# Turning attention probabilities by a product with a scaled diagonal, built on GpSimd

## The chip, the core and the metric

The kernel runs on one core of one Trainium2 chip. A core has five engines that run their own instruction streams and meet only through semaphores: PE (TensorE, matrix products; its weight loads are shown apart as PEld), DVE (VectorE), ACT (ScalarE), POOL (GpSimd) and SP (SyncE, which here only issues DMAs). The metric is the device time of one execution in microseconds; lower is better.

## What is computed

Two transformer blocks follow each other on 512 tokens of width 1024, all in float32. The second block holds the attention that this case is about. It has 16 query heads in 4 groups and three branches for each head: over 31 compressed keys ("c"), over selected blocks ("s") and over a window ("w"). With 512 tokens and 8 blocks of which 8 are chosen, "s" is plain causal attention, and "w" is causal attention with some padding keys. The core of it, from the reference:

```python
p_s = masked_softmax(s_s, key_pos <= t[:, None])
o_s = jnp.einsum('bghqkl,bgqkld->bghqd', p_s..., v_g)
...
p_w = masked_softmax(s_w, mask_w)
o_w = jnp.einsum('bghqk,bgkd->bghqd', p_w.astype(q_b.dtype), v_b)
return g_b[..., 0:1] * o_c + g_b[..., 1:2] * o_s + g_b[..., 2:3] * o_w
```

So every row of probabilities is an exponential, divided by its row sum, times a gate of that token, head and branch.

## The kernel before

The large matrix products (lines 888 to 890) split each float32 operand into two parts and take three products. They fill most of the time. The attention of the second block runs between 1661 and 1864 us of the span, in one software pipeline over the names "N0", "N1" and "X" (X is a cross attention that follows). N0 and N1 have two iterations each, and an iteration has 36 steps: 4 "c" steps, then 16 "s" and 16 "w" steps. A step is one head and one tile of 128 queries (`qt` from 0 to 3); its row is `e.n = 128 * (qt + 1)` keys wide, so widths of 128, 256, 384 and 512 come four steps each, twice per iteration. That makes 32 such steps and 80 chunks of 128 keys per iteration, 128 steps and 320 chunks in all.

What a step does, and on which engine:

- `score` (lines 743 to 748, PE): the product of q and k into a PSUM bank. Two heads stand next to each other in the array.
- `dve_attention`, first half (lines 841 to 849, DVE): adds the mask and takes the row's maximum, into `Sm` in SBUF.
- `act_attention` (lines 788 to 796, ACT): the exponential in place, with the row sum into `st[:, 12 + c]`.
- `dve_attention`, second half (lines 863 to 872, DVE), one step behind the first half: for "w" the padding's share is added to the sum (line 863), then the reciprocal (line 865), then line 872 multiplies the whole row of `Sm` by the reciprocal and by the gate, and increments `s_norm`.
- `turned_over` (lines 750 to 761, PE): waits for `s_norm`, turns each chunk of `Sm` with `pe.transpose` against the identity `ident` (a part of the tile `cst`) into one of two PSUM banks, and increments `t_full`.
- `act_attention` (line 813, ACT): copies the turned chunks to `PTnr` in SBUF.
- `values` (lines 763 to 767 and 1095, PE): the product with v, for two heads at once.

The order on PE is written out by hand: for each pair of steps, two scores, then a turn and a product with v, then a second turn and perhaps a second product with v. The turns stand three steps behind the scores (`lag_of` gets the whole name "N0" here, which isn't in "ANX"). `Sm` is a ring of six rows. POOL has nothing to do between its clearing of `PTc` (line 568) and the fetch of `xT` back from memory (line 572), which waits for the start of X.

Of the kernel before, what the change touches and what calls it, by code (L numbers as in the profile page):

```python
# [20 lines left out]
ACT = mybir.ActivationFunctionType  # L21
# [86 lines left out]
def build(nc, a, out):  # L108

    ctx = ExitStack()  # L110
    with ctx:
# [151 lines left out]
        ng = place("ng", [P, TT, 48])  # L263
        ngT = place("ngT", [48, T], at=S_at)
# [171 lines left out]
        bias_ready, pair_ready = sem("bias_ready"), sem("pair_ready")  # L436
# [61 lines left out]

        @block.gpsimd
        def _(pool):  # L500
            pool.memset(ones[:, :], 1.0).then_inc(pool_cst, 1)
            pool.memset(eps[:, :], EPS).then_inc(pool_cst, 1)
            pool.memset(kcT[:, :, :], 0.0).then_inc(pool_cst, 1)
            pool.memset(vcp[:, :, :], 0.0).then_inc(pool_cst, 1)

            pool.memset(diag[:, 0, 0:2], 0.0).then_inc(sq_used, 2)
            pool_squares(pool, 0)
            pool_squares(pool, 1)
            pool.wait_ge(cst_in, 16)

            for h in range(8 + 2):
                if h >= 2:
                    b = bias4[(h - 2) % 4]
                    if h < 6:

                        pool.wait_ge(o_free, O_RING + attn_at["B"]["O0"])
                    else:

                        pool.wait_ge(s_masked, attn_at["B"]["S0"] + 8 * ((h - 4) // 2))
                    pool.wait_ge(bias_in[h % 2], 16 * (h // 2))  # L520
                    pool.tensor_tensor(b[:, :], bias_raw[:, h % 2, :], C("mask_chunk"), ALU.add).then_inc(bias_ready, 1)
                if h < 8:
                    if h >= 2:

                        pool.wait_ge(bias_ready, h - 1)
                    pool.dma_start(bias_raw[:, h % 2, :], a["rel"][h]).then_inc(bias_in[h % 2], 16)
            pool_squares(pool, NORM["ffn2"])

            pool.wait_ge(sq_ready, 8 * NORM["final"] + 1)
            for m, a_ in enumerate((acc, acc_g)):  # L530
                pool.memset(a_[:, :], 0.0).then_inc(acc_zero, 1)
                pool.wait_ge(acc_zero, NORM["final"] + 1 + m)
            with pool.Fori(0, DC) as i:
                for s, a_ in enumerate((acc, acc_g)):
                    pool.wait_ge(sq_ready, i * 2 + (8 * NORM["final"] + s + 1))

                    pool.wait_ge(sq_used, i * 2 + (8 * NORM["final"] + s + 2))
                    pool.tensor_tensor(a_[:, :], a_[:, :], sqb[s][:, :], ALU.add).then_inc(sq_used, 1)

            pool.wait_ge(h_tmp, 8)  # L540
            pool.dma_start(spill, xT[:, :, :].rearrange("p c t -> p (c t)")).then_inc(spilled, 16)

            for m, n in enumerate("kv"):
                pool.dma_start(w1c[m][:, :, :], a[f"w_cmp_{n}1_2"][0].rearrange("(m p) n -> p m n", p=P)).then_inc(cmp_in, 16)
                pool.dma_start(w2c[:, m, :, :], a[f"w_cmp_{n}2_2"][0].rearrange("(c p) n -> p c n", p=P)).then_inc(cmp_in, 16)

            for m in range(2):
                for g in range(4):
                    pool.wait_ge(mm_free[2 * m + g // 2], 1 + stages["kc"]["m0"][2 * m + g // 2] + 1)
                    src = kcv[64 * (g % 2):64 * (g % 2) + 64, 2 * m + g // 2, :]  # L550
                    pool.dma_start(Z[m][0:64, g, :], src).then_inc(z_in[m], 16)
                    pool.dma_start(Z[m][64:128, g, 0:T - 1], src[:, 1:T]).then_inc(z_in[m], 16)

            pool.wait_ge(vc_done, 1)
            for m in range(2):
                pool.memset(wrg[m][:, :, :], 0.0).then_inc(wrg_zero, 1)
            pool.wait_ge(wrg_zero, 2)
            for m, n in enumerate("ai"):
                w = a[f"w_rg_{n}_2"][0].rearrange("(c b) i j -> b i c j", b=2)
                for b in range(2):  # L560
                    pool.dma_start(wrg[m][64 * b:64 * b + 64, :, 64 * b:64 * b + 64], w[b]).then_inc(rg_in, 16)


            pool.wait_ge(y1_done, DC)
            for h in range(4):
                if h:
                    pool.wait_ge(qz_zero, h)
                pool.memset(PTc[h][:, :], 0.0).then_inc(qz_zero, 1)

            pool.wait_ge(pv_done, PV_RING + attn_at["X"]["M0"])  # L570
            pool.wait_ge(spilled, 16)
            pool.dma_start(xT[:, :, :].rearrange("p c t -> p (c t)"), spill).then_inc(spill_back, 16)
            pool_squares(pool, NORM["g_mlp"])
            j = NORM["g_final"]
            pool.wait_ge(sq_ready, 8 * j + 1)
            pool.memset(acc[:, :], 0.0).then_inc(acc_zero, 1)
            pool.wait_ge(acc_zero, j + 1)
            for c in range(DC - 1):
                pool.wait_ge(sq_ready, 8 * j + c + 1)
                pool.wait_ge(sq_used, 8 * j + c + 2)  # L580
                pool.tensor_tensor(acc[:, :], acc[:, :], sqb[c % 2][:, :], ALU.add).then_inc(sq_used, 1)


        class Order:


            def __init__(self, eng, sem_):
                self.eng, self.sem, self.n, self.i, self.per = eng, sem_, 0, None, 0

            def __call__(self, ins):  # L590
                ins.then_inc(self.sem, 1)
                self.n += 1
                self.eng.wait_ge(self.sem, self.n if self.i is None else self.i * self.per + self.n)

            def loop(self, n, per, body):

                if n < 3:
                    for i in range(n):
                        at = self.n
                        body(i)  # L600
                        assert self.n == at + per, (self.n - at, per)
                else:
                    at = self.n
                    with self.eng.Fori(0, n) as i:
                        self.i, self.per = i, per
                        body(i)
                        assert self.n == at + per, (self.n - at, per)
                    self.i, self.n = None, at + n * per

        def full(S, b, i):  # L610

            return i + (S["m0"][b] + 1)

        def free_before(S, b, i):

            return i + (S["m0"][b] + 1)

        def free_after(S, b, i):

            return i + (S["m0"][b] + 2)  # L620

        def act_split(act, S, s, i):

            if S["name"] == LAST and isinstance(i, int) and i == S["its"] - 1:
                return
            act.wait_ge(w_raw[s], i * 16 + 16 * (S["k0"] + 2))
            if S["rel"][s] is None:
                act.wait_ge(slot0_used, i + (S["s0"] + 1))
            else:
                act.wait_ge(mm_full[S["rel"][s]], full(S, S["rel"][s], i))  # L630
            act.activation(whi[s][:, :], wraw[s][:, :], ACT.Copy).then_inc(w_hi[s], 1)  # L631

        def dve_split(dve, S, s, i):

            if S["name"] == LAST and isinstance(i, int) and i == S["its"] - 1:
                return
            dve.wait_ge(w_hi[s], i + (S["k0"] + 2))
            dve.tensor_tensor(wlo[s][:, :], wraw[s][:, :], f32(whi[s][:, :]), ALU.subtract).then_inc(w_lo[s], 1)  # L638

# [83 lines left out]

        def steps(names):

            at = [(n, i, t) for n in names for i in range(attn_at[n]["its"]) for t in range(attn_at[n]["n"])]  # L730
            bank0 = PREP[{"A": "ak", "B": "bk", "C": "cq", "N0": "kk"}[names[0]]][1]
            return [Step(n, i, t, k, bank0) for k, (n, i, t) in enumerate(at)], lag_of(names[0])

        def pe_attention(pe, names, q_of, k_of, v_of, turn, chunk_of):
# [16 lines left out]
            def turned_over(e):  # L751

                pe.wait_ge(s_norm, e.s + 1)
                pe.wait_ge(t_free, e.u + 1)
                if e.m == "c":
                    for q in range(TT):
                        mm = pe.transpose(e.tbank[0:NC32, q * P:(q + 1) * P], e.Sm[:, q * NC32:(q + 1) * NC32], ident)
                else:
                    for kc in range(e.n // P):
                        mm = pe.transpose(e.tbank[:, kc * P:(kc + 1) * P], e.Sm[:, kc * P:(kc + 1) * P], ident)  # L760
                mm.then_inc(t_full, 1)
# [1563 lines left out]
```

## Time and profile before

| what | value |
|---|---|
| median of 3 runs | 2375.66 us (2374.99 to 2376.89) |
| time of the profiled execution | 2375.66 us |
| span of the profiled execution, first to last instruction | 2373.5 us |
| mean granted TensorE clock | 0.983 of full speed |
| PE, PEld, DVE, ACT, POOL busy, share of the span | 96%, 76%, 52%, 41%, 6% |
| one iteration of the 36 steps, from the chain | 46.34 us, four of them |

The span leaves out 2.2 us ahead of the first and behind the last instruction. Busy time of PE counts each product from its start to its modelled end, and products overlap; so the distance from one start to the next is what a product costs, not its duration.

### The profile page before, as it was taken

The numbers are of one execution on the slowest core, as the hardware profiler recorded it, in microseconds if no ns is written. First come the engines' busy times: TensorE is split into PE (matmuls) and PEld (weight loads), VectorE is DVE, ScalarE is ACT, GpSimd is POOL, SyncE is SP. The second block draws the span as 40 slices with busy tenths as digits, with TensorE's granted clock in tenths as the row PEclk, the third lists the DMA queues.
The fourth block names the chain that finished last, engine by engine and source line by source line (L and its number), as shares of the span: only waits on it lengthen the run. The fifth ranks groups of instructions, "written<-read, shape, count | busy, mean of one in ns | idle before, by whom it ended". The sixth has DMA issues, their size and how long they took to land.

```text
span 2373.5 us, 29956 instructions
## 1 busy us (share of the span) xinstructions
PE 2276.7 (96%) x10990; PEld 1805.0 (76%) x10990; DVE 1235.4 (52%) x2245; ACT 976.4 (41%) x1620; POOL 147.7 (6%) x119
## 2 busy tenths in 40 slices
PE   7999999989889999999999999999999999999998
PEld 6888888757667777888888877687555788888887
DVE  6444436674545455434434656743899655432432
ACT  6332224454555333433223422633788544321322
POOL 2000002101000000100001420000000001000011
PEclk9999999989899999999999999999999999999999
DMA  6322323212101223232322372122000232333231
GB/s 234 106 90 87 107 92 102 98 54 64 61 27 54 80 98 106 89 106 83 112 88 76 102 250 70 61 92 75 2 2 2 72 107 95 100 91 104 89 106 54
DMA packets 213615, 206.81 MB, mean 87 GB/s; under 512 B 4848, under 2 KB 194544, under 8 KB 213264
## 3 DMA queue, kind: packets, MB, share of 16 engines
q1 hardware_dynamic: 210512, 192.31, 25.6%
q0 software_dynamic: 3008, 13.24, 1.7%
q8 instruction: 59, 0.97, 0.2%
q14 instruction: 36, 0.29, 0.0%
HBM read 199.25 MB, written 4.19 MB: 86 GB/s over the span
## 4 chain that ended last, share of the span: by engine, by line
PE 82%; DVE 8%; ACT 5%; issue 3%; DMA 1%; POOL 0%; ACTq 0%; SPq 0%; DVEq 0%; POOLq 0%
PE ps L888 25%; PE ps L890 25%; PE ps L889 25%; DVE Sm L843 2%; DVE wlo L638 2%; PE ps L748 2%; PE ps L760 2%; ACT whi L631 2%; PE ps L1095 1%; DMA wraw<-in_w_in 1%; DVE st L865 1%; PE ps L1087 1%; PE ps L1135 1%; PE ps L1160 1%; DVE Sm L872 0%
## 5 line engine op out<-in xcount | busy, mean ns | idle before, releaser
L888 PE MATMUL ps<-hH,whi 128*128 128x512 f32 x1528 | 600.8, 393 | 15.6 <-DVE wlo L638 13.8
L638 DVE TENSOR_TENSOR wlo<-wraw,whi 128x2048 fp32r<-128x2048 f32 x192 | 440.4, 2294 | 324.0 <-ACT whi L631 324.0
L890 PE MATMUL ps<-hH,wlo 128*128 128x512 f32 x1528 | 596.0, 390 | 0.0
L889 PE MATMUL ps<-hL,whi 128*128 128x512 f32 x1528 | 595.8, 390 | 0.0
L631 ACT ACTIVATE whi<-wraw 128x2048 fp32r<-128x2048 f32 x192 | 366.8, 1911 | 436.4 <-PE ps L890 428.6
L888 PEld LDWEIGHTS ps<-hH,whi 128*128 128x128 f32 x1528 | 287.1, 188 | 83.6 <-issue 14.5
L889 PEld LDWEIGHTS ps<-hL,whi 128*128 128x128 f32 x1528 | 287.0, 188 | 61.3 <-issue 1.4
L890 PEld LDWEIGHTS ps<-hH,wlo 128*128 128x128 f32 x1528 | 287.0, 188 | 60.8
L888 PE MATMUL ps<-gH,whi 128*128 128x512 f32 x608 | 237.2, 390 | 0.0
L889 PE MATMUL ps<-gL,whi 128*128 128x512 f32 x608 | 236.6, 389 | 0.0
L890 PE MATMUL ps<-gH,wlo 128*128 128x512 f32 x608 | 236.6, 389 | 0.0
L888 PE MATMUL ps<-whi,hH 128*128 128x512 f32 x352 | 138.9, 395 | 9.4 <-ACT tk L1425 4.5
L889 PE MATMUL ps<-wlo,hH 128*128 128x512 f32 x352 | 137.6, 391 | 0.0
L890 PE MATMUL ps<-whi,hL 128*128 128x512 f32 x352 | 137.6, 391 | 0.0
L796 ACT ACTIVATE Sm<-Sm,st 128x128 f32<-128x128 f32 (+3 forms) x224 | 122.8, 548 | 25.9 <-DVE st L843 24.3
L890 PEld LDWEIGHTS ps<-gH,wlo 128*128 128x128 f32 x608 | 114.1, 188 | 23.8
L889 PEld LDWEIGHTS ps<-gL,whi 128*128 128x128 f32 x608 | 114.1, 188 | 23.6
L888 PEld LDWEIGHTS ps<-gH,whi 128*128 128x128 f32 x608 | 114.1, 188 | 23.5
L760 PEld LDWEIGHTS ps<-cst,Sm 128*128 128x128 f32 x504 | 55.8, 144 | 99.5 <-DVE Sm L872 34.4
L760 PE MATMUL ps<-cst,Sm 128*128 128x128 f32 x504 | 100.0, 301 | 29.3 <-DVE Sm L869 12.5
L843 DVE CUSTOM_DVE_ANT_0 Sm<-ps,cst 128x256 f32<-128x256 f32 (+3 forms) x192 | 90.9, 474 | 19.9 <-PE ps L748 17.8
L1359 ACT ACTIVATE gH<-prod 128x512 f32 x44 | 27.8, 632 | 171.5 <-DVE prod L1779 171.5
(340 smaller groups left out, 2675.5 us busy)
## 6 DMA issues: line engine op xcount, KB each, us to landing
wraw<-in_w_in SPq DMA_DIRECT2D x45, 1024.0 KB, 5.0
wraw<-in_ffn_wg SPq DMA_DIRECT2D x22, 1024.0 KB, 5.1
wraw<-in_ffn_wu SPq DMA_DIRECT2D x22, 1024.0 KB, 5.2
wraw<-in_w_up SPq DMA_DIRECT2D x16, 1024.0 KB, 5.2
wraw<-in_w_down SPq DMA_DIRECT2D x16, 1024.0 KB, 5.1
wraw<-in_ffn_wd SPq DMA_DIRECT2D x16, 768.0 KB, 4.3
wraw<-in_w_gate SPq DMA_DIRECT2D x12, 1024.0 KB, 4.9
wraw<-in_ffn_wd SPq DMA_DIRECT2D x16, 640.0 KB, 4.0
```

The lines of the kernel that those rows point to most:

```text
L631: act.activation(whi[s][:, :], wraw[s][:, :], ACT.Copy).then_inc(w_hi[s], 1)
L638: dve.tensor_tensor(wlo[s][:, :], wraw[s][:, :], f32(whi[s][:, :]), ALU.subtract).then_inc(w_lo[s], 1)
L748: mm = pe.matmul(e.bank[:, 0:e.n], q_of(e, e.qt), k_of(e, e.n), start=True, stop=True)
L760: mm = pe.transpose(e.tbank[:, kc * P:(kc + 1) * P], e.Sm[:, kc * P:(kc + 1) * P], ident)
L796: act.activation(e.Sm[:, 0:e.n], e.Sm[:, 0:e.n], ACT.Exp, bias=st[:, 8 + e.c:9 + e.c], scale=-1.0, accum_out=st[:, 12 + e.c:13 + e.c]).the ...
L843: scored = dve.tensor_tensor_reduce(s_[:, 0:n], e.bank[:, 0:n], mask_of(e, n), -1.0, 0.0 if e.m == "w" and e.qt < TT - 1 else 3e38, ALU.ad ...
L865: order(dve.reciprocal(st[:, 16 + c:17 + c], st[:, 12 + c:13 + c]))
L888: pe.matmul(o, lh, rh, start=start, stop=False)
L889: pe.matmul(o, lh, rl, start=False, stop=False)
L890: return pe.matmul(o, ll, rh, start=False, stop=stop)
L1087: mm = nc.tensor.matmul(ob[:, q * P:(q + 1) * P], src[:, kc, q * P:(q + 1) * P], Vt[:, kc, at:at + P], start=kc == 0, stop=kc == q)
L1359: act.activation(gH[:, i * 2 + g, :], prod[g][:, :], ACT.Copy).then_inc(g_hi, 1)
```

## The change

It touches the 128 "s" and "w" steps of N0 and N1; "c", X and the first block's attentions stay. Line 872's multiplication of the row goes. DVE's part of the step ends at the reciprocal, which now increments `s_norm`. POOL waits for that, and writes into one of four tiles `dg` (128 x 128) the identity times the reciprocal times the gate, both being one number for each partition. It increments `dg_ready`. PE's turn waits for `dg_ready` and, in place of the transpose against the identity, takes a product of the chunk (as the stationary operand) with this diagonal. The result is the turned and scaled chunk. From the fifth diagonal on, POOL waits for the turn that used the same tile of `dg` (`t_full`), and DVE waits with its reciprocal until the diagonal that read the same number of `st` is made. `nsa_gate` is the former `gate_of`, moved. The diff shows the whole POOL block as moved further down; nothing else in it changes.

```diff
+        dg = place("dg", [P, 4, P], at=arena + 22528)
...
+        def diagonal_no(e):
+
+            if e.kind != "N" or e.m == "c":
+                return None
+            at = e.s - attn_at["N0"]["S0"]
+            return at // 36 * 32 + at % 36 - 4
...
+            turns = [None] * 4
+            for e in steps(["N0", "N1"])[0]:
+                d = diagonal_no(e)
+                if d is None:
+                    continue
+                pool.wait_ge(s_norm, e.s + 1)
+                if d >= 4:
+
+                    pool.wait_ge(t_full, turns[d % 4] + 1)
+                turns[d % 4] = e.u
+                pool.tensor_scalar(dg[:, d % 4, :], ident, st[:, 16 + e.c:17 + e.c], nsa_gate(e), ALU.mult, ALU.mult).then_inc(dg_ready, 1)
...
             def turned_over(e):
 
-                pe.wait_ge(s_norm, e.s + 1)
+                d = diagonal_no(e)
+                if d is not None:
+                    pe.wait_ge(dg_ready, d + 1)
+                else:
+                    pe.wait_ge(s_norm, e.s + 1)
                 pe.wait_ge(t_free, e.u + 1)
+                if d is not None:
+                    for kc in range(e.n // P):
+                        mm = pe.matmul(e.tbank[:, kc * P:(kc + 1) * P], e.Sm[:, kc * P:(kc + 1) * P], dg[:, d % 4, :], start=True, stop=True)
+                    mm.then_inc(t_full, 1)
+                    return
...
+                        d = diagonal_no(e)
+                        if d is not None:
+                            if d >= 4:
+
+                                dve.wait_ge(dg_ready, d - 3)
+                            dve.reciprocal(st[:, 16 + c:17 + c], st[:, 12 + c:13 + c]).then_inc(s_norm, 1)
+                            continue
                         order(dve.reciprocal(st[:, 16 + c:17 + c], st[:, 12 + c:13 + c]))
...
-                        elif e.kind == "N":
-                            dve.tensor_scalar(s_[:, 0:n], s_[:, 0:n], st[:, 16 + c:17 + c], gate_of(e),
-                                              ALU.mult, ALU.mult).then_inc(s_norm, 1)
```

## Rows read from the trace of the kernel before

**Rows 1.** The page: busy time, share of the span, instructions of each engine.

```profile
PE 2276.7 (96%) x10990; PEld 1805.0 (76%) x10990; DVE 1235.4 (52%) x2245; ACT 976.4 (41%) x1620; POOL 147.7 (6%) x119
```

**Rows 2.** Stretches: PE, PEld, DVE, ACT, POOL busy (instructions); clock, DMA share, GB/s.

```profile
1717.70:1764.10 46.40, 43.77 (x363) 26.25 (x361) 41.95 (x181) 37.30 (x124) 0.00 (x0) 1.00 0.01 1
...
1718.60:1735.70 17.10, 16.98 (x149) 10.41 (x147) 15.50 (x64) 15.48 (x52) 0.00 (x0) 1.00 0.01 1
1735.70:1749.60 13.90, 11.90 (x86) 6.11 (x82) 12.99 (x57) 10.86 (x41) 0.00 (x0) 1.00 0.01 2
```

**Rows 3.** Waits from 1665 to 1850 us: total us, times, longest.

```profile
PEld ps L760 <- DVE Sm L872: 34.4, 58, 1.3
...
PE ps L760 <- DVE Sm L872: 8.0, 9, 1.1
```

**Rows 4.** PE over time within one iteration: start us, us to modelled end.

```profile
1722.28 1.10 PE L760 MATMUL ps<-cst,Sm 128*128 128x128 f32 x5
...
1736.64 0.83 PE L760 MATMUL ps<-cst,Sm 128*128 128x128 f32 x3
...
1740.57 0.44 PE L760 MATMUL ps<-cst,Sm 128*128 128x128 f32 x2
1741.86 0.55 PE L760 MATMUL ps<-cst,Sm 128*128 128x128 f32 x3 [0.84 <-DVE Sm L872]
...
1746.58 0.55 PE L760 MATMUL ps<-cst,Sm 128*128 128x128 f32 x3
1748.22 0.66 PE L760 MATMUL ps<-cst,Sm 128*128 128x128 f32 x4 [1.09 <-DVE Sm L872]
1748.81 0.88 PE L1095 MATMUL ps<-PTnr,v 128*64 128x128 f32 x12
...
1754.55 0.66 PE L760 MATMUL ps<-cst,Sm 128*128 128x128 f32 x4
1755.55 0.61 PE L757 MATMUL ps<-cst,Sm 128*32 128x128 f32 x4 [0.35 <-DVE Sm L860]
...
1757.12 0.49 PE L748 MATMUL ps<-kT,q 64*128 64x128 f32 x4
1757.54 0.61 PE L757 MATMUL ps<-cst,Sm 128*32 128x128 f32 x4
...
1760.92 0.33 PE L760 MATMUL ps<-cst,Sm 128*128 128x128 f32 x1
1761.18 1.08 PE L1114 MATMUL ps<-PTc,vcp 128*64 128x512 f32 x4
```

**Rows 5.** Groups from 1640 to 1870 us: busy us, mean ns, idle before and releasers.

```profile
L760 PE MATMUL ps<-cst,Sm 128*128 128x128 f32 x352 | 67.3, 294 | 9.7 <-DVE Sm L872 8.0 <-DVE Sm L875 0.6
L872 DVE TENSOR_SCALAR Sm<-Sm,st,ng 128x128 f32<-128x128 f32 (+3 forms) x128 | 57.1, 446 | 4.7
L748 PE MATMUL ps<-kT,q 64*128 64x128 f32 (+3 forms) x256 | 52.7, 489 | 0.0
```

**Rows 6.** PE over time in another stage, a plain float32 product.

```profile
1413.06 7.30 PE L1135 MATMUL ps<-RB,w1c 128*128 128x124 f32 x64
```

**Rows 7.** POOL's groups over the whole span: busy us, mean ns, idle before.

```profile
L501 POOL MEMSET ones<- 128x128 f32 x1 | 0.2, 204 | 0.3 <-POOLq L2321 0.3
L521 POOL TENSOR_TENSOR bias<-bias_raw,cst 128x512 f32<-128x512 f32 x8 | 10.4, 1302 | 211.5 <-ACT oT L820 124.4 <-DVE st L843 85.4 <-DMA bias_raw<-in_rel 1.7
L538 POOL TENSOR_TENSOR acc<-acc,sqb 128x512 f32<-128x512 f32 x8 | 21.1, 2632 | 16.5 <-ACT sqb L1379 16.2 <-POOL acc_g L531 0.3
```

**Rows 8.** DVE around one step: start us, us.

```profile
1738.62 0.17 DVE L865 RECIPROCAL st<-st 128x1 f32<-128x1 f32 x1
1738.82 0.41 DVE L872 TENSOR_SCALAR Sm<-Sm,st,ng 128x256 f32<-128x256 f32 x1
```

**Rows 9.** The chain of waits in order of time: start us, us.

```profile
1718.08 0.68 PE ps L748 x4
...
1764.42 0.68 PE ps L748 x4
```

More of the change, by code:

```diff
@@ L435, in build @@
         t_full, t_free, pv_done, o_free = (sem(x) for x in ("t_full", "t_free", "pv_done", "o_free"))
-        bias_ready, pair_ready = sem("bias_ready"), sem("pair_ready")
+        bias_ready, pair_ready, dg_ready = sem("bias_ready"), sem("pair_ready"), sem("dg_ready")
         oa_sq, oa_sd, oa_ready = (sem(x) for x in ("oa_sq", "oa_sd", "oa_ready"))
@@ L497, in pool_squares @@
                     pool.tensor_tensor(acc[:, :], acc[:, :], sqb[s][:, :], ALU.add).then_inc(sq_used, 1)
[L499 to L581, printed above, removed]
@@ L584, in build @@
[L584 to L608, printed above, removed]
@@ L610, in full @@
[L610 to L638, printed above, removed]
         def paired(kind):
@@ L726, in pt_free, with nsa_gate @@
                 return self.M + PV_RING - (3 if paired(self.kind) else 1)
+        def nsa_gate(e):
+            col = 3 * ((2 * int(e.name[1]) + e.h // 2) * 4 + 2 * e.i + e.h % 2) + "csw".index(e.m)
+            return ng[:, :, col] if e.qt is None or e.m == "c" else ng[:, e.qt, col:col + 1]
+        def diagonal_no(e):
[3 more added lines that the diff above has]
+            return at // 36 * 32 + at % 36 - 4
         def steps(names):
@@ L732, in steps, with _ @@
             return [Step(n, i, t, k, bank0) for k, (n, i, t) in enumerate(at)], lag_of(names[0])
+        @block.gpsimd
+        def _(pool):
+            pool.memset(ones[:, :], 1.0).then_inc(pool_cst, 1)
+            pool.memset(eps[:, :], EPS).then_inc(pool_cst, 1)
+            pool.memset(kcT[:, :, :], 0.0).then_inc(pool_cst, 1)
+            pool.memset(vcp[:, :, :], 0.0).then_inc(pool_cst, 1)
+            pool.memset(diag[:, 0, 0:2], 0.0).then_inc(sq_used, 2)
+            pool_squares(pool, 0)
+            pool_squares(pool, 1)
+            pool.wait_ge(cst_in, 16)
+            for h in range(8 + 2):
+                if h >= 2:
+                    b = bias4[(h - 2) % 4]
+                    if h < 6:
+                        pool.wait_ge(o_free, O_RING + attn_at["B"]["O0"])
+                    else:
+                        pool.wait_ge(s_masked, attn_at["B"]["S0"] + 8 * ((h - 4) // 2))
+                    pool.wait_ge(bias_in[h % 2], 16 * (h // 2))
+                    pool.tensor_tensor(b[:, :], bias_raw[:, h % 2, :], C("mask_chunk"), ALU.add).then_inc(bias_ready, 1)
+                if h < 8:
+                    if h >= 2:
+                        pool.wait_ge(bias_ready, h - 1)
+                    pool.dma_start(bias_raw[:, h % 2, :], a["rel"][h]).then_inc(bias_in[h % 2], 16)
+            pool_squares(pool, NORM["ffn2"])
+            pool.wait_ge(sq_ready, 8 * NORM["final"] + 1)
+            for m, a_ in enumerate((acc, acc_g)):
+                pool.memset(a_[:, :], 0.0).then_inc(acc_zero, 1)
+                pool.wait_ge(acc_zero, NORM["final"] + 1 + m)
+            with pool.Fori(0, DC) as i:
+                for s, a_ in enumerate((acc, acc_g)):
+                    pool.wait_ge(sq_ready, i * 2 + (8 * NORM["final"] + s + 1))
+                    pool.wait_ge(sq_used, i * 2 + (8 * NORM["final"] + s + 2))
+                    pool.tensor_tensor(a_[:, :], a_[:, :], sqb[s][:, :], ALU.add).then_inc(sq_used, 1)
+            pool.wait_ge(h_tmp, 8)
+            pool.dma_start(spill, xT[:, :, :].rearrange("p c t -> p (c t)")).then_inc(spilled, 16)
+            for m, n in enumerate("kv"):
+                pool.dma_start(w1c[m][:, :, :], a[f"w_cmp_{n}1_2"][0].rearrange("(m p) n -> p m n", p=P)).then_inc(cmp_in, 16)
+                pool.dma_start(w2c[:, m, :, :], a[f"w_cmp_{n}2_2"][0].rearrange("(c p) n -> p c n", p=P)).then_inc(cmp_in, 16)
+            for m in range(2):
+                for g in range(4):
+                    pool.wait_ge(mm_free[2 * m + g // 2], 1 + stages["kc"]["m0"][2 * m + g // 2] + 1)
+                    src = kcv[64 * (g % 2):64 * (g % 2) + 64, 2 * m + g // 2, :]
+                    pool.dma_start(Z[m][0:64, g, :], src).then_inc(z_in[m], 16)
+                    pool.dma_start(Z[m][64:128, g, 0:T - 1], src[:, 1:T]).then_inc(z_in[m], 16)
+            pool.wait_ge(vc_done, 1)
+            for m in range(2):
+                pool.memset(wrg[m][:, :, :], 0.0).then_inc(wrg_zero, 1)
+            pool.wait_ge(wrg_zero, 2)
+            for m, n in enumerate("ai"):
+                w = a[f"w_rg_{n}_2"][0].rearrange("(c b) i j -> b i c j", b=2)
+                for b in range(2):
+                    pool.dma_start(wrg[m][64 * b:64 * b + 64, :, 64 * b:64 * b + 64], w[b]).then_inc(rg_in, 16)
+            pool.wait_ge(y1_done, DC)
+            for h in range(4):
+                if h:
+                    pool.wait_ge(qz_zero, h)
+                pool.memset(PTc[h][:, :], 0.0).then_inc(qz_zero, 1)
+            turns = [None] * 4
[8 more added lines that the diff above has]
+                pool.tensor_scalar(dg[:, d % 4, :], ident, st[:, 16 + e.c:17 + e.c], nsa_gate(e), ALU.mult, ALU.mult).then_inc(dg_ready, 1)
+            pool.wait_ge(pv_done, PV_RING + attn_at["X"]["M0"])
+            pool.wait_ge(spilled, 16)
+            pool.dma_start(xT[:, :, :].rearrange("p c t -> p (c t)"), spill).then_inc(spill_back, 16)
+            pool_squares(pool, NORM["g_mlp"])
+            j = NORM["g_final"]
+            pool.wait_ge(sq_ready, 8 * j + 1)
+            pool.memset(acc[:, :], 0.0).then_inc(acc_zero, 1)
+            pool.wait_ge(acc_zero, j + 1)
+            for c in range(DC - 1):
+                pool.wait_ge(sq_ready, 8 * j + c + 1)
+                pool.wait_ge(sq_used, 8 * j + c + 2)
+                pool.tensor_tensor(acc[:, :], acc[:, :], sqb[c % 2][:, :], ALU.add).then_inc(sq_used, 1)
@@ new lines, in build, with __init__, __call__, loop @@
+        class Order:
+            def __init__(self, eng, sem_):
+                self.eng, self.sem, self.n, self.i, self.per = eng, sem_, 0, None, 0
+            def __call__(self, ins):
+                ins.then_inc(self.sem, 1)
+                self.n += 1
+                self.eng.wait_ge(self.sem, self.n if self.i is None else self.i * self.per + self.n)
+            def loop(self, n, per, body):
+                if n < 3:
+                    for i in range(n):
+                        at = self.n
+                        body(i)
+                        assert self.n == at + per, (self.n - at, per)
+                else:
+                    at = self.n
+                    with self.eng.Fori(0, n) as i:
+                        self.i, self.per = i, per
+                        body(i)
+                        assert self.n == at + per, (self.n - at, per)
+                    self.i, self.n = None, at + n * per
@@ new lines, in full, with free_before, free_after, act_split @@
+        def full(S, b, i):
+            return i + (S["m0"][b] + 1)
+        def free_before(S, b, i):
+            return i + (S["m0"][b] + 1)
+        def free_after(S, b, i):
+            return i + (S["m0"][b] + 2)
+        def act_split(act, S, s, i):
+            if S["name"] == LAST and isinstance(i, int) and i == S["its"] - 1:
+                return
+            act.wait_ge(w_raw[s], i * 16 + 16 * (S["k0"] + 2))
+            if S["rel"][s] is None:
+                act.wait_ge(slot0_used, i + (S["s0"] + 1))
+            else:
+                act.wait_ge(mm_full[S["rel"][s]], full(S, S["rel"][s], i))
+            act.activation(whi[s][:, :], wraw[s][:, :], ACT.Copy).then_inc(w_hi[s], 1)
@@ L734, in pe_attention, with dve_split @@
+        def dve_split(dve, S, s, i):
+            if S["name"] == LAST and isinstance(i, int) and i == S["its"] - 1:
+                return
+            dve.wait_ge(w_hi[s], i + (S["k0"] + 2))
+            dve.tensor_tensor(wlo[s][:, :], wraw[s][:, :], f32(whi[s][:, :]), ALU.subtract).then_inc(w_lo[s], 1)
         def pe_attention(pe, names, q_of, k_of, v_of, turn, chunk_of):
@@ L751, in turned_over @@
             def turned_over(e):
-                pe.wait_ge(s_norm, e.s + 1)
-                pe.wait_ge(t_free, e.u + 1)
+                d = diagonal_no(e)
+                if d is not None:
+                    pe.wait_ge(dg_ready, d + 1)
+                else:
+                    pe.wait_ge(s_norm, e.s + 1)
+                pe.wait_ge(t_free, e.u + 1)
+                if d is not None:
+                    for kc in range(e.n // P):
+                        mm = pe.matmul(e.tbank[:, kc * P:(kc + 1) * P], e.Sm[:, kc * P:(kc + 1) * P], dg[:, d % 4, :], start=True, stop=True)
+                    mm.then_inc(t_full, 1)
+                    return
                 if e.m == "c":
@@ L2188, in _ @@
             dve.wait_ge(turn_free, PREP["kk"][1] + 4)
-            def gate_of(e):
-                col = 3 * ((2 * int(e.name[1]) + e.h // 2) * 4 + 2 * e.i + e.h % 2) + "csw".index(e.m)
-                return ng[:, :, col] if e.qt is None or e.m == "c" else ng[:, e.qt, col:col + 1]
             dve_attention(dve, order, ["N0", "N1", "X"],
-                          lambda e, n: C("mask_chunk")[:, 0:n] if e.kind == "X" else C("mask_causal")[:, T - n:T], gate_of)
+                          lambda e, n: C("mask_chunk")[:, 0:n] if e.kind == "X" else C("mask_causal")[:, T - n:T], nsa_gate)
             dve_split(dve, S, 1, 0)
```

## The prediction

> **What bounds the kernel now.** I read the page's first part, then the stretches of the attention stage, then the waits in it, and last PE's own order of time.
>
> The page says PE is busy for 96% of the span, and nothing else comes near [rows 1]. So outside the touched stage any time moved on PE shifts the end one for one, and time moved on DVE or ACT alone doesn't. In the stage the four iterations repeat; the chain passes the same score at 1718.08 and 1764.42, so one takes 46.34 us [rows 9]. In that time PE is busy 43.7 us, DVE 41.9 and ACT 37.2, at full clock (1.00, that is 2.4 GHz) [rows 2]. Two engines are close to the limit. The halves differ: in the "s" stretch PE is busy 16.98 of 17.10 us, in the "w" stretch only 11.90 of 13.90 us while DVE is busy 12.99 [rows 2]. So "s" is bound by PE, and "w" in part by DVE.
>
> How much does PE wait for DVE? The table of waits gives two answers: the weight loads wait 34.4 us for line 872, the products 8.0 us in 9 waits [rows 3]. The first is misleading, since a weight load waits "for DVE" while the products of the last score still run. I count starts instead. A turn of one chunk takes 0.26 us from its first product to the next group's (1760.92 to 1761.18) and one of four 0.59 (1748.22 to 1748.81) [rows 4]; so a chunk is 0.11 us, and two and three chunks take 0.37 and 0.48. A turn that directly follows a turn costs 0.11 a chunk. From 1740.57 to 1741.86 pass 1.29 us for a turn of two, which needs 0.28: 1.0 lost. From 1746.58 to 1748.22 pass 1.64 us where 0.39 are needed: 1.25 lost [rows 4]. Two merged rows hold smaller waits: five chunks last 1.10 us to their modelled end where four last 0.66 and one more should add 0.11, and three last 0.83 where 0.55 is usual [rows 4]: 0.3 lost in each. That is 2.9 us per iteration. In the "c" steps line 860 is waited for: 1.00 us from 1754.55 to 1755.55 for a turn that needs 0.59 [rows 4], 0.4 lost, and I put smaller ones there at 0.3. So PE alone would need 46.34 - 3.6 = 42.7 us per iteration, and 14 us is all that a perfect DVE could give back in four.
>
> **The change part by part.**
>
> DVE loses 128 multiplications: 17.5 + 15.3 + 13.2 + 11.1 = 57.1 us [rows 5], 14.3 per iteration. It also no longer waits out the reciprocal, which today costs 0.20 us from its start to the next instruction (1738.62 to 1738.82) [rows 8]. DVE falls from 41.9 to under 28 us per iteration. It stops being a bound, and the 2.9 us of waits for line 872 go but for a rest that I put at 0.3: a gain of 2.6. The 0.7 in the "c" steps come in part because DVE arrives late from the "w" steps; I take 0.4 of them as gained. On PE that is -3.0 per iteration (bounds: 0, if GpSimd's answer is as late as DVE's, and -3.6).
>
> PE's turn becomes a plain float32 product. The trace shows what that means. The 320 chunks of N and 32 of X are 352 instructions at line 760: a transpose is one instruction [rows 5]. The 128 scores are 256 instructions: a plain float32 product is two [rows 5]. The nearest row for size is line 1135, 128 x 128 weights and 124 moving columns: 64 instructions in 7.30 us, less one tail of 0.28, over 63, is 0.1115 us each [rows 6]. So a chunk costs 0.223 us in place of 0.11. The first of a group costs more, since its second weight load isn't hidden: a score of width 128, two instructions on two halves of the array side by side, takes 0.42 us to the next group (1757.12 to 1757.54) [rows 4], where a one-chunk transpose takes 0.26. Turns of 1 to 4 chunks then take 0.42, 0.64, 0.87 and 1.09 us, which is 0.16, 0.27, 0.39 and 0.50 more. Eight of each per iteration: 8 x 1.32 = 10.5 us. Without any such start cost it is 80 x 0.113 = 9.0 us. Six of the 32 turns follow another turn without a gap and have no start cost, so I take 9.9.
>
> Here a rule of the Trainium skill speaks against the change. The page "TensorE: Matmul & The Clock Gate", section "Terms", says that trn2's matmul has a transpose mode which is four times faster for FP32. The trace shows the direction, but twice and not four times the instructions, at nearly the same 0.11 us each; what four times would give is the last rival.
>
> GpSimd gets 128 small operations, on an engine that is idle in the stage [rows 2]. No row shows this operation. From below, a memset of the same 128 x 128 takes 0.20 us; from above, two-input operations of four times the width take 1.30 to 2.63 us on average [rows 7]. A quarter of these is 0.33 and 0.66. I take 0.5, between the two, and keep 0.20 to 2.63 as the ends. Is it on the path? What it replaces in the latency is line 872, which ends 0.2 + 0.41 = 0.6 us after the reciprocal's start [rows 8]; now it is 0.17 for the reciprocal plus 0.5. About equal, and a turn stands three steps behind its score on PE, so nothing is added: 0. If it costs 2.63, 32 of them are 84 us per iteration, and POOL becomes the bound (below).
>
> A sentence on the page's price: "GPSIMD Engine Reference", section "Elementwise — side-by-side cycle accounting", puts the best loop at about 1.8 cycles per element at 1.2 GHz, which would be an estimate of 0.19 us for 128 elements, ahead of dispatch. No run shows it for this operation, and the sum would be the same by it.
>
> The new waits. POOL waits for the turn four diagonals back; behind it in its queue stand only further diagonals, and then the fetch of `xT`, which waits for X anyway. DVE's reciprocal waits for the diagonal four back; behind it stands the next mask, so a late POOL would hold back scores too. At 0.5 us against 1.4 us per step neither is ever last. ACT's work is unchanged, 37.2 us in a longer iteration. On entering X DVE has no backlog, which saves perhaps 0.5 us once.
>
> **The sum.** Per iteration +9.9 - 3.0 = +6.9 us; four give 27.6, less 0.5: +27. The profiled execution took 2375.66 us (span 2373.5 and 2.2 around it), the same as the median. So 2403 us, 1.1% slower. With 9.0 and -3.6 it is +21, 2397; with 10.5 and 0 it is +42, 2418.
>
> **Rivals.**
>
> *DVE's release pays for the product (not slower).* If the 34.4 us that weight loads wait for line 872 were truly lost time, they would come back together with the 8.0 of the products, 42 against 4 x 9.9 = 40: 2373 us, no change. It decides from 40 us of regained waits on. For it: the row is the largest wait of the stage. Against: PE is busy 43.7 of 46.34 us, so 34.4 + 8.0 us can't be idle in four iterations that have 14. It would need product groups that overlap much better behind a ready operand than today's. Chance 0.05.
>
> *The product is no dearer than the transpose (faster).* If the diagonal product ran at one instruction per chunk, only the regained waits would be left: 4 x 3.0 = 12, 2363 us. Against it, every plain float32 product here is doubled. Chance 0.04. The change doesn't do what it says in this case: no added PE time.
>
> *GpSimd becomes the bound (slower still).* From about 1.3 us per diagonal on, a narrow step's turn would wait for it: at some 0.5 us for each of 8 narrow turns, +16 us on the sum, 2419. At 2.63 us POOL paces the 32 steps: 84 us plus some 10 of "c" steps against 53, +41 x 4, 2567 us. For it: 2.63 us rows exist, where another engine seems to hinder POOL. Against: a quarter of the width. Chance 0.08.
>
> *The product costs four transposes.* 0.44 us per chunk: 80 x 0.33 = 26.4, less 3.0, four times: +94, 2469 us. The page named above would give this. Rows 6 speaks against it. Chance 0.02.
>
> **How the numbers follow.** The forecast has 0.81: 2403 us. The range 2391 to 2418 takes in the bounds 2397 and 2418 and some room below for turns that lose their start cost; outside it lie the two faster rivals, four transposes, and most of a late GpSimd, together under 0.2. About 0.2% is what a measurement of this kernel can tell from no change, 4.8 us. Faster by more: 0.05. Within: 0.05. Slower: 0.90.
>
> **What would show it.** At the turn's line 640 products instead of 320, at 0.11 us from start to start; an iteration of 53.2 us instead of 46.34; DVE busy near 28 of it; PE without a wait of 1 us at the wide "w" turns; POOL 128 operations of 0.4 to 0.7 us; the rest of the kernel unchanged. Wrong would be: long waits of PE for POOL (rival three), or an iteration under 47 us with 640 products (rival one).

## The result and the profile after

The changed kernel takes 2401.77 us (median of 4 runs, 2398.34 to 2405.41) against 2376.27 us of the kernel before beside it: a ratio of 1.0107, with a 95% interval of 1.009 to 1.0125. It is slower by 25.5 us. The forecast was 2403, in a range of 2391 to 2418.

The span of the profiled execution grew from 2373.5 to 2401.0 us, 27.5 us. By the starts of products that both kernels share, 1.5 us of it came before the attention stage (the first product with `kcT` starts at 1655.96 us before and at 1657.49 after), 25.5 us in the stage, up to the last product of X with v, and 0.5 us behind it. What came before the stage is not put down to the change: both kernels run the same instructions there, the granted clock of the first block's attention varies from run to run (0.75 from 500 to 560 us before, 0.71 after), and in three runs of the experiments below the stage starts at 1654.4, 1656.2 and 1658.4 us.

The page and the stretches of after; the stretches' columns are those of [rows 2], the first is one iteration, the second and third are the same work as the "s" and "w" stretch there:

```profile
PE 2315.8 (96%) x11310; PEld 1852.0 (77%) x11310; DVE 1189.6 (50%) x2117; ACT 972.4 (40%) x1620; POOL 205.9 (9%) x247
...
1722.90:1775.60 52.70, 52.68 (x442) 37.48 (x443) 30.43 (x148) 36.01 (x123) 14.45 (x32) 1.00 0.01 2
1726.90:1748.70 21.80, 21.80 (x189) 15.85 (x187) 10.15 (x52) 15.27 (x52) 6.66 (x15) 1.00 0.01 2
1748.70:1763.20 14.50, 14.50 (x110) 9.76 (x108) 10.31 (x47) 10.97 (x41) 4.63 (x11) 1.00 0.01 2
```

PE is busy for 52.68 of 52.70 us: there is no gap left. The "s" stretch, which PE already filled [rows 2], grew by 4.7 us, from 17.10 to 21.80. The "w" stretch, which had the long waits, grew only from 13.90 to 14.50. The other 1.0 us of the iteration lies in the rest, between the "w" stretch and the next "s" stretch. DVE went from 41.95 to 30.43 us and POOL from 0 to 14.45.

The chain of after, where it passes the same score of three iterations (start us, us), gives the iteration as 52.7 us, against 46.34 before [rows 9]:

```profile
1723.94 0.63 PE ps L772 x4
...
1776.63 0.63 PE ps L772 x4
...
1829.34 0.63 PE ps L772 x4
```

Four times 6.36 is 25.4 us, the whole growth of the stage. The groups of the stage (busy us, mean ns, idle before) and PE over time in the "s" stretch:

```profile
L785 PE MATMUL ps<-dg,Sm 128*128 128x128 f32 x640 | 97.9, 291 | 0.0
L681 POOL TENSOR_SCALAR dg<-cst,st,ng 128x128 f32<-128x128 f32 x128 | 57.8, 452 | 256.9 <-DVE st L903 251.8 <-PE ps L785 5.1
```

```profile
1729.06 0.71 PE L785 MATMUL ps<-dg,Sm 128*128 128x128 f32 x4
1729.70 0.44 PE L1132 MATMUL ps<-PTnr,v 128*64 128x128 f32 x4
...
1734.52 0.94 PE L785 MATMUL ps<-dg,Sm 128*128 128x128 f32 x6
1735.38 0.66 PE L1132 MATMUL ps<-PTnr,v 128*64 128x128 f32 x8
```

The 320 chunks are 640 products, at no idle time. The second row puts 5.1 us of POOL's idle time down to PE; that is not so, as is said below under GpSimd. A turn of two chunks now takes 0.64 us to the next group's start (1729.06 to 1729.70) and one of three 0.86 (1734.52 to 1735.38), where 0.37 and 0.48 were needed before.

The waits of after, over the stage: total us, times, longest.

```profile
POOL dg L681 <- DVE st L903: 251.8, 120, 111.4
ACT PTnr L846 <- PE ps L785: 59.5, 81, 2.0
DVE Sm L876 <- PE ps L772: 52.1, 61, 2.1
PEld ps L785 <- POOL dg L681: 20.2, 32, 0.8
...
PE ps L790 <- DVE Sm L893: 0.8, 1, 0.8
```

The last row is the only wait of PE itself. The 20.2 us of the weight loads cost nothing, since the products of the group before still run. The direction has turned. Before, PE waited for DVE [rows 3]; now ACT and DVE wait for PE.

### The profile page after: what moved, and what is told of

Its sections match the earlier page's. It is cut to its first block, busy times and chain, and to the rows that moved or that the text cites. A ratio compares the mean times of both kernels' runs of the same rounds, so it can differ in the third digit from the quotient of the medians.

```text
span 2401.0 us, 30846 instructions
## 1 busy us (share of the span) xinstructions
PE 2315.8 (96%) x11310; PEld 1852.0 (77%) x11310; DVE 1189.6 (50%) x2117; ACT 972.4 (40%) x1620; POOL 205.9 (9%) x247
## 4 chain that ended last, share of the span: by engine, by line
PE 88%; DVE 4%; ACT 4%; issue 1%; DMA 1%; POOL 0%; ACTq 0%; SPq 0%; DVEq 0%; POOLq 0%
PE ps L925 25%; PE ps L927 24%; PE ps L926 24%; PE ps L785 4%; PE ps L772 3%; PE ps L1132 2%; DVE wlo L751 2%; ACT whi L744 2%; DMA wraw<-in_w_in 1%; PE ps L793 1%; PE ps L1172 1%; PE ps L1124 1%; DVE Sm L876 1%; PE ps L1197 1%; PE ps L770 0%
## 5 line engine op out<-in xcount | busy, mean ns | idle before, releaser
L925 PE MATMUL ps<-hH,whi 128*128 128x512 f32 x1528 | 601.0, 393 | 15.6 <-DVE wlo L751 13.8
L785 PEld LDWEIGHTS ps<-dg,Sm 128*128 128x128 f32 x640 | 79.2, 191 | 36.3 <-POOL dg L681 20.2
L785 PE MATMUL ps<-dg,Sm 128*128 128x128 f32 x640 | 97.9, 291 | 0.0
```

The lines of the kernel that those rows point to most:

```text
L785: mm = pe.matmul(e.tbank[:, kc * P:(kc + 1) * P], e.Sm[:, kc * P:(kc + 1) * P], dg[:, d % 4, :], start=True, stop=True)
L925: pe.matmul(o, lh, rh, start=start, stop=False)
```

## The experiments

The question was whether the right total had come from the right terms: 9.9 us of products, 3.0 us of regained waits, nothing for GpSimd. "Iteration" is the distance between equal products of two iterations in each run's own trace; it is free of what the first block does. Line 872 below is the line of the kernel before, and the kernels before that ran beside an experiment had medians of 2377.5 to 2381.7 us. The totals differ from their neighbours by several us outside the stage too, so sizes are read from the iteration: the product alone is 19.3 us above its neighbours, while its iteration says 4 x 6.63 = 26.5.

### The product alone

```diff
-                        mm = pe.transpose(e.tbank[:, ...], e.Sm[:, ...], ident)
+                        turn_ = pe.matmul if e.kind == "N" else pe.transpose
+                        kw = dict(start=True, stop=True) if e.kind == "N" else {}
+                        mm = turn_(e.tbank[:, ...], e.Sm[:, ...], ident, **kw)
```

> The kernel before, with one edit: the 128 turns of N0 and N1 are plain products with the identity instead of transposes. VectorE still scales the rows, GpSimd does nothing. It computes the same thing. Theory (TensorE's own work sets the stage once the products are in): VectorE needs 42 us of an iteration that grows to 52.7, so its waits disappear without its work being touched; iteration 52.5 to 53.5 us, total 2400 to 2404 us, the same as the changed kernel. Rival (the prediction's sum read literally: product +9.9, and VectorE's relief is what takes the 3.0 of waits away): iteration 56.2, total about 2415 us.

Measured: 2400.04 us, ratio 1.0094 (1.0068 to 1.0119), iteration 52.97 us. One iteration, in the columns of [rows 2]:

```profile
1719.80:1772.70 52.90, 52.90 (x440) 37.56 (x440) 42.76 (x180) 36.75 (x123) 0.00 (x0) 1.00 0.01 2
```

DVE still does all its work, 42.76 us, and PE shows no gap; only two pairs of turns in the "w" stretch take 0.19 and 0.09 us longer than in after. So nearly the whole loss is there with this one edit, and the other half of the change, which takes work off DVE, is worth 0.27 us per iteration, about 1 us in all. The rival, the sum read literally, fell.

### DVE's relief alone

```diff
+                        if e.kind == "N":
+                            dve.reciprocal(st[:, 16 + c:17 + c], st[:, 12 + c:13 + c]).then_inc(s_norm, 1)
+                            continue
```

> The kernel before without line 872 and with nothing in its place: the rows of the s and w steps are not scaled at all (that part of the computation is left out), the turns stay transposes. It measures what VectorE's relief is worth by itself. Theory: the 2.9 us of waits for line 872 go and some of the 0.7 in the c steps, iteration 43.0 to 43.6 us, total 2362 to 2366 us. Rival (the 34.4 us that weight loads wait for line 872 are lost time): total 2335 to 2342 us.

Measured: 2363.94 us, ratio 0.9933 (0.9915 to 0.9951), iteration 42.80 us. With transposes the relief is worth 3.54 us per iteration, 14 in all, and what is left is nearly all PE's own time:

```profile
1714.10:1756.90 42.80, 42.63 (x360) 26.31 (x361) 30.24 (x148) 36.13 (x123) 0.00 (x0) 1.00 0.01 2
```

PE's floor, which the prediction put at 42.7, is a little lower still, for two waits are left in this iteration. A turn of three and one of four chunks together need 0.91 us (1726.50 to 1727.41) and took 1.11 (1744.16 to 1745.27), and another 0.17 us are spent waiting for ACT:

```profile
1714.11 1.08 PE L1117 MATMUL ps<-PTc,vcp 128*64 128x512 f32 x4 [0.17 <-ACT yn L820]
...
1726.50 0.98 PE L760 MATMUL ps<-cst,Sm 128*128 128x128 f32 x7
1727.41 0.88 PE L1098 MATMUL ps<-PTnr,v 128*64 128x128 f32 x12
...
1744.16 1.18 PE L760 MATMUL ps<-cst,Sm 128*128 128x128 f32 x7
1745.27 0.88 PE L1098 MATMUL ps<-PTnr,v 128*64 128x128 f32 x12
```

That makes the floor 42.4 us, and a kernel further down reaches it with 42.43. Against the floor, the products of the changed kernel cost 52.70 - 42.43 = 10.3 us; against this run it would be 9.90.

### The diagonal made and waited for, but not used

```diff
-                        mm = pe.matmul(e.tbank[:, ...], e.Sm[:, ...], dg[:, d % 4, :], start=True, stop=True)
+                        mm = pe.transpose(e.tbank[:, ...], e.Sm[:, ...], ident)
```

> The changed kernel with transposes against the identity in place of the products: GpSimd still makes every diagonal and every turn waits for it, but it is not used, so the scaling is left out. Against the run without scaling it shows what GpSimd's latency costs when TensorE is at its fastest. Theory: 0.17 for the reciprocal and 0.45 for the diagonal are no later than line 872 was, so at most 0.5 us per iteration: 43.0 to 44.0 us, total 2362 to 2368 us. Rival (a hidden GpSimd latency that the longer products cover in the changed kernel): iteration 45 us or more, total 2372 or more.

Measured: 2369.3 us, ratio 0.9954 (0.9938 to 0.997), iteration 44.28 us: 1.48 more than without GpSimd, where I expected at most 0.5, and less than the rival's 45. PE's waits in it:

```profile
PE ps L785 <- POOL dg L681: 3.4, 8, 0.5
```

So GpSimd's answer is late when the turns are short; its latency lies on the path there. Still it is 2.06 us per iteration better than DVE's rows.

### Each diagonal made two and four times

```diff
+                pool.tensor_scalar(dg[:, d % 4, :], ident, ...).then_inc(dg_more, 1)
+                pool.wait_ge(dg_more, 1 * d + 1)
                 pool.tensor_scalar(dg[:, d % 4, :], ident, ...).then_inc(dg_ready, 1)
```

> The changed kernel, but GpSimd makes each diagonal twice (the second waits for the first), so that its answer takes about 0.95 us in place of 0.45. Theory (the products keep TensorE busy while the diagonal is made): at most 0.5 us per iteration on the 52.70, total 2398 to 2404 us. Rival (the diagonal lies on the path): half a microsecond at each of the 32 turns, 16 us per iteration at most, total above 2412.

> The same with each diagonal made four times in a row, about 1.9 us per step against 1.47 us that a step has. Here GpSimd must be the bound: 32 times 1.9 is 61 us for the s and w steps and some 5 of c steps beside them, iteration 62 to 68 us, total 2438 to 2465. Rival (the queues hide it too): under 2410.

Measured, twice: 2409.0 us, ratio 1.0123 (1.0096 to 1.015), iteration 54.45. That is 1.75 us more than 52.70, between the theory and the rival: 0.55 us more at each of 32 turns would be 17.6 us, and a tenth of it shows. Four times: 2487.14 us, iteration 74.8 and 75.2. GpSimd is the bound, as expected, but the size was off. Its operations with the wait between them follow each other at 0.55 us, not at 0.45 to 0.48:

```profile
1745.28 0.45 POOL L681 TENSOR_SCALAR dg<-cst,st,ng 128x128 f32<-128x128 f32 x1
1745.83 0.45 POOL L683 TENSOR_SCALAR dg<-cst,st,ng 128x128 f32<-128x128 f32 x1
1746.38 0.45 POOL L685 TENSOR_SCALAR dg<-cst,st,ng 128x128 f32<-128x128 f32 x1
1746.93 0.45 POOL L687 TENSOR_SCALAR dg<-cst,st,ng 128x128 f32<-128x128 f32 x1
1747.36 0.45 POOL L681 TENSOR_SCALAR dg<-cst,st,ng 128x128 f32<-128x128 f32 x1
```

That is 2.08 us per step, 67 for 32 steps. The rest is about 8 us, of which POOL waits 7.7 us for reciprocals, 5.93 in one piece around the "c" steps. PE's granted clock was 0.89 in this iteration; what that added to the time, these runs don't separate.

```profile
1741.60:1816.40 74.80, 62.41 (x441) 42.40 (x440) 30.84 (x148) 36.66 (x123) 57.60 (x128) 0.89 0.00 1
```

### The change in one half of the steps

The diagonal, the product and the missing multiplication for the chosen steps only; the others as before.

```diff
+            chosen = [x for x in range(4, 36) if x >= 20]
+            if at % 36 not in chosen:
+                return None
```

> The diagonal and the product for the 16 w steps of an iteration only; the 16 s steps as before. Same result as the reference. Theory: half of the products, +4.9 us, and the waits of the w stretch, 2.6 of 2.9 us, go: iteration 48.4 to 49.0 us, total 2384 to 2387 us. Rival (the waits are not where VectorE is late but spread over both stretches): iteration 49.8 or more, total 2389 or more.

> Diagonal and product for the 16 s steps only, w steps as before. Same result as the reference. Theory: the products add 4.9 us and take with them only the waits of the s stretch (0.3 us) and perhaps half a microsecond in c steps, those of the w stretch stay: iteration 50.3 to 51.2 us, more than the 48.18 of the w steps alone, total about 2393 to 2396. Rival (the price depends on the number of products alone): 48.2 as in the w steps.

Measured, "w" only: 2383.45 us, ratio 1.0016 (1.0003 to 1.003), iteration 48.18, a little better than expected. "s" only: 2393.82 us (one run), iteration 51.33, a little worse than expected. Both halves have 40 chunks. The first was expected from 48.4 us, the second up to 51.2. The same products cost 1.84 us per iteration where DVE was late and 4.99 us where PE already was full. PE's waits in the second one show that those of the "w" stretch stayed:

```profile
PE ps L796 <- DVE Sm L915: 7.7, 8, 1.1
```

### GpSimd scales rows, with transposes

If the product is the loss and DVE's lateness the thing to mend, GpSimd can scale the rows itself. First for the eight narrow "w" steps of an iteration. The turns are transposes again, DVE scales the other rows, and POOL's wait for an earlier turn goes with the ring of diagonals:

```diff
-                pool.tensor_scalar(dg[:, d % 4, :], ident, st[:, 16 + e.c:17 + e.c], nsa_gate(e), ALU.mult, ALU.mult).then_inc(dg_ready, 1)
+                pool.tensor_scalar(e.Sm[:, 0:e.n], e.Sm[:, 0:e.n], st[:, 16 + e.c:17 + e.c], nsa_gate(e), ALU.mult, ALU.mult).then_inc(dg_ready, 1)
```

> The kernel before (transposes, rows scaled), but GpSimd scales the rows of the w steps of width 128 and 256, 8 of 32 per iteration, in place; VectorE scales the others. Same result as the reference. Theory: VectorE falls behind in the w stretch because it needs 12.99 of 13.90 us there; eight rows less (0.35 to 0.41 us each and 0.1 of waiting out the reciprocal) are 3.8 us, so the two waits of 1.0 and 1.25 us at the wide w turns go. Iteration 43.6 to 44.6 us, total 2364 to 2370 us. Rival (GpSimd's latency, which cost 1.5 us per iteration in the run with unused diagonals, makes new waits of the same size): iteration 46 us or more, total 2374 or more.

Measured: 2379.07 us, ratio 1.0004 (0.9987 to 1.0021), iteration 45.89. Of the two long waits the first fell from 0.84 to 0.29 us and the other, at the first turn of width 512, stayed at 1.09. Relief in the narrow steps doesn't reach the wide ones: with it, DVE waits for PE's next score, up to 0.56 us at a time, in place of getting ahead, and from width 384 on it works without a gap again (lines 848 and 849 add two operations at width 512). PE's two rows:

```profile
1745.98 0.55 PE L792 MATMUL ps<-cst,Sm 128*128 128x128 f32 x3 [0.29 <-DVE Sm L911]
...
1752.35 0.66 PE L792 MATMUL ps<-cst,Sm 128*128 128x128 f32 x4 [1.09 <-DVE Sm L911]
```

Theory and rival both missed: the rival's 46 us or more was nearer, but its cause, waits for GpSimd, is not what the trace shows.

### One more step of distance

```diff
-            return [Step(n, i, t, k, bank0) for k, (n, i, t) in enumerate(at)], lag_of(names[0])
+            return [Step(n, i, t, k, bank0) for k, (n, i, t) in enumerate(at)], lag_of(names[0][0])
```

> The kernel before with the turns four steps behind the scores instead of three, nothing else. Same result as the reference. Theory: the waits for line 872 come from a VectorE that is about 1.3 us late, not from one that is too slow over an iteration (41.9 of 46.3 us), so one more step of distance hides most of them: iteration 43.5 to 45 us, total 2363 to 2370. Rival (VectorE's throughput in the w stretch sets it, whatever the distance): iteration 45.8 or more, total 2373 or more.

Measured: 2374.92 us, ratio 0.9979 (0.9966 to 0.9992), iteration 46.06. The rival held: with DVE's rows in place the distance hides next to nothing. PE itself no longer waits for line 872 but for ACT's copies of turned chunks, and ACT in turn waits for DVE's mask in the wide "w" steps (line 849; 9.8 us in all):

```profile
PE ps L760 <- ACT PTnr L813: 5.6, 11, 0.7
```

### Both: GpSimd scales all rows, at three and at four steps

> GpSimd scales every s and w row in place (reciprocal times gate), VectorE none; turns stay transposes, three steps behind the scores. Same result as the reference. In the run with eight narrow rows GpSimd took 0.45 us for a row of 128 and 0.55 for one of 256, so 0.10 per 128 more: 0.66 and 0.77 for 384 and 512. Theory (the loss of the change is the product alone; what GpSimd adds is a latency of 0.45 to 0.77 us at each turn): a little more than the 44.28 us per iteration with unused diagonals of 0.45 us, 44.5 to 45.3 us; total 7 to 4 us below the kernel before. Rival (in-place rows of 512 on GpSimd hinder VectorE or come too late): iteration 46.3 or more, no gain.

> The same, with the turns four steps behind the scores. Same result as the reference. Theory: GpSimd's latency, which cost 1.5 us per iteration with the unused diagonals, is hidden by one more step of distance; iteration 42.8 to 43.8 us, total 10 to 14 us below the kernel before (0.4 to 0.6%). Rival (the distance costs TensorE something of its own, as the run with four steps and VectorE's rows, 46.06 against 46.34, suggests): 44.3 or more, no better than with three steps.

Measured at three steps: 2370.44 us, ratio 0.9956 (0.9941 to 0.997), iteration 45.13 in the stretch with full clock; the two before it took 46.75 and 49.80 us at granted clocks of 0.96 and 0.90. At four: 2360.91 us, ratio 0.9914 (0.9901 to 0.9928), iteration 42.43. This computes the same as both kernels and beats them: 21 us below the kernel before that ran beside it, some 40 below the changed one. By the iteration it is 4 x 3.91 = 15.6 us below the kernel before; the other 5 us lie outside the iterations and are not shown to be of this edit. GpSimd's groups and one iteration of it:

```profile
L680 POOL TENSOR_SCALAR Sm<-Sm,st,ng 128x512 f32<-128x512 f32 x32 | 24.7, 772 | 19.7 <-DVE st L902 19.7
L680 POOL TENSOR_SCALAR Sm<-Sm,st,ng 128x384 f32<-128x384 f32 x32 | 21.3, 666 | 12.9 <-DVE st L902 12.9
L680 POOL TENSOR_SCALAR Sm<-Sm,st,ng 128x256 f32<-128x256 f32 x32 | 17.8, 558 | 16.7 <-DVE st L902 16.4
L680 POOL TENSOR_SCALAR Sm<-Sm,st,ng 128x128 f32<-128x128 f32 x32 | 14.4, 451 | 148.4 <-DVE st L902 148.4
```

```profile
1713.90:1756.30 42.40, 42.40 (x363) 26.31 (x362) 30.64 (x148) 35.23 (x123) 19.57 (x32) 1.00 0.01 2
```

PE is full again, at the transposes' price. The distance that brought nothing with DVE's rows brings 2.7 us per iteration here: at three steps PE waited 6.2 us for GpSimd in 12 waits, at four not once. What it hides is a latency and not a lack of throughput.

### The change with four steps of distance

The distance edit on top of the changed kernel.

> The changed kernel (diagonals and products) with the turns four steps behind the scores. Same result as the reference. Theory (with the products TensorE has no waits left that distance could hide; it was busy 52.68 of 52.70 us): iteration 52.2 to 52.9 us, total 2396 to 2403 us, so the step that brought the version with GpSimd's rows from 45.13 to 42.43 us per iteration brings nothing here. Rival (the changed kernel too pays for GpSimd's latency, as the run with every diagonal made twice hints): iteration 51.5 or less, total below 2395.

Measured: 2402.33 us, ratio 1.0106 (1.0078 to 1.0133), iteration 52.57 against 52.70. As expected: the changed kernel has no wait for distance to hide.

## Why the prediction was right

**PE's floor.** Counting starts instead of reading the weight loads' 34.4 us gave 42.7 us; the run without scaling measured 42.80, and 42.4 without the waits left in it. The count of PE's waits was 0.3 us short of that. This step carried the forecast, since it ruled out the rival in which DVE's release pays for the product. That rival, like the cheap product and the fourfold product, is refuted by the rows of after: 640 products, and no idle time before them.

**The product.** The price of a turn was right: line 1135's 0.1115 us and the score's 0.42 us [rows 4, 6] gave 0.64 and 0.87 us for two and three chunks, and 0.64 and 0.86 were measured. Why the first product of a group costs more was argued there and is tested by no run. The addition was not right: 10.5 us less six start costs of 0.05 are 10.2, and the prediction took 9.9. Counting every turn of one iteration from start to start in both traces gives 10.2 too, with seven turns that directly follow another, and the floor gives 10.3. That 52.70 - 42.80 comes to just 9.90 is luck. The fourfold price of the page "TensorE: Matmul & The Clock Gate" of the Trainium skill, section "Terms", doesn't show in this kernel: a chunk costs two instructions where it cost one.

**The regained waits: too small, and the wrong cause.** -3.0 us were booked to DVE's relief. The run with the product alone has DVE's full work and yet only 52.97 us. The waits went because PE became the slower engine. Either edit removes them, so they can be counted once and for either. And all of them went: PE waited once, for 0.8 us, in the whole stage, so 46.34 - 42.43 = 3.9 us per iteration were regained. The prediction left 0.6 us of the waits that it had found in place and had missed 0.3. So +10.3 - 3.9 = +6.4 us stand against its +9.9 - 3.0 = +6.9: two terms that were both too small, by 0.4 and 0.9 us, and in part cancel. The forecast of 2403 us is nearer than its terms. The 0.5 us that it took off once, for entering X without a backlog, did not come either: four iterations account for 25.4 of the 25.5 us by which the stage grew.

**DVE's work.** It fell to 30.4 us, not under 28. I subtracted the 57.1 us of durations [rows 5], but a multiplication's end overlapped the next instruction's start (line 872 from 1738.82 for 0.41 us, the next instruction at 1739.14), so its removal frees less busy time than its duration. Nothing hung on it.

**GpSimd.** 0.5 us were taken, 0.452 measured. "Nothing is added" holds only under the products' cover. With short turns the same diagonals cost 1.5 us per iteration, and 0.55 us more per diagonal costs 1.75 under the products. The latency was nearer to the path than the comparison with line 872 said. That comparison left out the hand-over: in the trace of after every one of the 128 diagonals starts 0.09 to 0.11 us after its reciprocal's end. That holds for the eight too which the profile puts down to PE, 5.1 us in sum; one of them, with its reciprocal:

```profile
1736.71 0.16 DVE L903 RECIPROCAL st<-st 128x1 f32<-128x1 f32 x1 [0.57 <-ACT Sm L829]
...
1736.97 0.45 POOL L681 TENSOR_SCALAR dg<-cst,st,ng 128x128 f32<-128x128 f32 x1 [0.88 <-PE ps L785]
```

So POOL's new wait for the turn four diagonals back was never the last to end, as predicted.

**The rest of the kernel** was unchanged but for 2 us outside the stage, of the size by which its start differs between runs.

## What to carry to other kernels

Before moving work off a late engine onto the full one, find the full engine's own time by counting from start to start with the waits taken out; here 42.7 of 46.34 us said that a perfect VectorE was worth 14 us (15.6 with the floor as measured) and no product could be paid from it. Waits are regained once: when the engine that waits gets slower, they vanish by themselves, and a gain booked for ending them is no gain. A transpose that becomes a float32 product costs two instructions for one, so scaling inside the turn is dear, while an idle GpSimd scales the rows themselves for a latency that one more step of distance hides.

## What the hardware showed that was not expected

GpSimd's float32 row scaling, one tensor input and two numbers per partition, took 0.451, 0.558, 0.666 and 0.772 us at widths of 128, 256, 384 and 512: 0.107 us per 128 columns and about 0.34 fixed. DVE took 0.346 to 0.546 for the same rows [rows 5 has the mean, 446 ns]. So GpSimd was between 1.3 and 1.4 times as slow, and its row of 512 took 0.77 us where the two-input operations of [rows 7] take 1.30 to 2.63 us. The Trainium skill, "GPSIMD Engine Reference", section "Elementwise — side-by-side cycle accounting", gives 1.03 cycles per element as the port's bound for short loop bodies. The trace agrees: at the page's 1.2 GHz the slope here is an estimated 1.0 cycle.

In the kernel with every diagonal made four times the granted clock of one iteration was 0.89 of full speed, with PE idle for 12 of 75 us; in the changed kernel it was 1.00. But it also fell where PE had hardly been idle. The kernel with GpSimd's rows at three steps ran one iteration at 0.90, with PE busy for 48.01 of 49.80 us, and the next at 1.00 in 45.10:

```profile
1714.30:1764.10 49.80, 48.01 (x360) 30.10 (x361) 30.82 (x148) 36.22 (x123) 19.45 (x32) 0.90 0.01 2
1764.10:1809.20 45.10, 43.33 (x360) 26.31 (x360) 30.52 (x148) 36.19 (x123) 19.44 (x32) 1.00 0.01 2
```

These are the same instructions, 4.7 us apart. What made the clock fall there, no run shows; it is a reason to compare iterations at the same granted clock.
